# A two-block transformer step on one core: the conditioning products moved to TensorE, the first norm done by token, the last bias joined to the expert products, and an earlier next block

## The reference, cut to what matters

```python
mod = silu(c) @ w_ada + b_ada                      # one row of 6 * 1024, six parts
h = rms(x, norm_mix) * (1 + sc_m) + sh_m           # needs sh_m, sc_m: the first 2048 columns
proj = h @ w_in                                    # q, kv, q_i, k_i, w_i, z, xbc, dt, gates
mixed = sigmoid(g_attn) * y_attn + sigmoid(g_ssd) * y_ssd
x = x + g_m * (mixed @ w_out)
h = rms(x, norm_ffn) * (1 + sc_f) + sh_f
# 32 experts, 4 per token: for each row of a block of expert e
out = act(xb @ w_gu[e] + b_gu[e]) @ w_dn[e] + b_dn[e]
x = x + g_f * sum over the token's experts of gate * out
```

## Time and profile before

| what | value |
|---|---|
| three runs | 2173.53, 2178.62, 2182.28 us; median 2178.62 us |
| the profiled execution, its own time | 2177.95 us |
| its span, from the first to the last instruction | 2176.1 us |
| mean granted TensorE clock | 0.966 |
| busy: PE, PEld, DVE, ACT, POOL | 1990.9, 1168.7, 679.1, 368.4, 75.7 us |
| moved by DMA | 583.21 MB, 268 GB/s over the span |

### The profile page before, as it was taken

The page is one execution under the profiler, slowest core; times in us unless marked ns, Lnnn a source line. Parts: engine busy times, 40 slices in busy tenths (PEclk is TensorE's granted clock), DMA queues, the critical chain, the costliest instruction groups (busy, mean ns, idle before and its releaser), DMA issues.

```text
span 2176.1 us, 22293 instructions
## 1 busy us (share of the span) xinstructions
PE 1990.9 (91%) x8838; PEld 1168.7 (54%) x8838; DVE 679.1 (31%) x1352; ACT 368.4 (17%) x747; POOL 75.7 (3%) x132
## 2 busy tenths in 40 slices
PE   3987899899998998988999898898999999999998
PEld 2774786533333333333333333566788547668863
DVE  6499541422221112211122221252333015423321
ACT  1122311201010000000010100233211023422110
POOL 0000000000000000000000000110000011000000
PEclk8998989799999999999999999899999999999999
DMA  9674424499999999999999996452444332334441
GB/s 355 208 246 177 154 78 177 190 399 427 427 427 428 428 428 428 428 428 427 428 429 427 428 428 286 174 187 84 163 150 150 132 140 94 138 119 152 155 155 39
DMA packets 135538, 583.21 MB, mean 268 GB/s; under 512 B 9432, under 2 KB 55640, under 8 KB 110640
## 3 DMA queue, kind: packets, MB, share of 16 engines
q1 hardware_dynamic: 131424, 575.87, 66.3%
q0 software_dynamic: 4048, 6.42, 1.4%
HBM read 579.64 MB, written 2.62 MB: 268 GB/s over the span
## 4 chain that ended last, share of the span: by engine, by line
PE 58%; DMA 30%; DVE 8%; ACT 2%; issue 2%; SPq 1%; PEldq 0%; DVEq 0%; PEld 0%; ACTq 0%
PE psum L351 45%; DMA work<-w_gu 17%; DMA work<-w_dn 9%; PE psum L561 8%; PE psum L604 4%; DVE work L1363 2%; DMA ring<-w_gu 1%; DMA ring<-w_dn 1%; DMA ring<-w_ada 1%; PE psum L1877 1%; DVE work L1565 1%; DMA ring<-w_in 1%; SPq L455 0%; PE psum L932 0%; DVE work L1535 0%
## 5 line engine op out<-in xcount | busy, mean ns | idle before, releaser
L351 PE MATMUL psum<-normed,ring 128*128 128x256 f32 (+1 forms) x2432 | 507.9, 371 | 4.9 <-DMA ring<-w_in 4.9
L351 PEld LDWEIGHTS psum<-normed,ring 128*128 128x128 f32 x2432 | 444.3, 192 | 65.3 <-DMA ring<-w_in 5.2
L561 PE MATMUL psum<-ring,normed 128*64 128x512 f32 x1024 | 236.6, 617 | 33.5 <-DMA ring<-w_gu 33.5
L561 PE MATMUL psum<-work,normed 128*64 128x512 f32 x1024 | 234.2, 612 | 33.9 <-DMA work<-w_gu 33.9
L351 PE MATMUL psum<-ring,work 128*128 128x512 f32 x560 | 242.3, 593 | 4.7 <-DVE work L2477 2.7
L351 PE MATMUL psum<-work 128*128 128x128 f32 (+8 forms) x1192 | 202.8, 349 | 21.2 <-issue 10.8
L351 PEld LDWEIGHTS psum<-work 128*128 128x128 f32 (+3 forms) x1192 | 149.6, 198 | 83.4 <-issue 62.2
L351 PE MATMUL psum<-ring,normed 128*128 128x512 f32 (+2 forms) x416 | 173.7, 575 | 13.4 <-DMA ring<-w_in 5.5
L561 PEld LDWEIGHTS psum<-ring,normed 128*64 128x64 f32 x1024 | 81.9, 142 | 187.9 <-issue 187.9
L561 PEld LDWEIGHTS psum<-work,normed 128*64 128x64 f32 x1024 | 81.6, 141 | 185.3 <-issue 185.3
L351 PEld LDWEIGHTS psum<-ring,work 128*128 128x128 f32 x560 | 105.9, 190 | 134.8 <-issue 132.7
(11 more groups left out here) (290 smaller groups left out, 1317.5 us busy)
## 6 DMA issues: line engine op xcount, KB each, us to landing
ring<-w_gu SPq DMA_DIRECT2D x64, 2048.0 KB, 27.1
work<-w_gu SPq DMA_DIRECT2D x64, 2048.0 KB, 27.2
ring<-w_dn SPq DMA_DIRECT2D x32, 2048.0 KB, 27.4
work<-w_dn SPq DMA_DIRECT2D x32, 2048.0 KB, 27.3
ring<-w_in SPq DMA_DIRECT2D x25, 2048.0 KB, 12.6
ring<-w_up SPq DMA_DIRECT2D x44, 1024.0 KB, 6.5
ring<-w_ada SPq DMA_DIRECT2D x12, 2048.0 KB, 15.9
ring<-w_down SPq DMA_DIRECT2D x10, 2048.0 KB, 7.8
```

Of the source, the lines that this page charges most:

```text
L351: return pe.matmul(out, lhsT, rhs, start=first, stop=last, **kw)
L561: ins = pe.matmul(b[r], self.hgT[:, 2 * q + k, r], ws[e][:, k, n0:n0 + 512], start=False, stop=q == QUARTERS - 1 and k == 1, skip_group_ch ...
```

## The change

- The 12 parts of `w_ada` are multiplied on PE: `ada(j)` makes eight products with `cond` as the stationary operand, 32 columns wide (one column is `cond`, the others are zero), the product of block k in rows 32 * (k mod 4) of one bank. ACT evicts the 128 x 512 result to `acc`, and `sum_mod` or `mod_rows` adds over the partitions as before. Parts 2, 3, 0, 1 come first. `sum_first` puts all four sums into one bank, which DVE evicts once. PE waits for its own products before it signals the slot used.
- The first norm goes by token: `x` is loaded once, ahead of `w_ada`, and stays; ACT and DVE scale it, PE turns it into four banks, and ACT and DVE evict the banks with scale and shift to `h`. `xT`, `sum_squares` and `inverse_root` are gone.
- `dt` is computed with the index weights (88 columns instead of 72); its own product is gone. The index scores, the masks and the picking of tile 0 go over 128 keys.
- PE's order: the gates `ga` 0 and 1 and both halves of `z` 1 are put between the logits and the attention of tile 1; the other gates go between the parts of the state-space part. The orders of ACT and of both lists are changed to match. DVE scales `y` of tile 0 before it starts on tile 1.
- `x1` waits for `mixed` by pairs of blocks. The ranks are counted by tile, in three banks. The rows of a pair are announced in two halves.
- `GT`, `yb`, and their four scalings and additions are gone. Each pair has two more products of two rows, `b_dn`, that start the banks of the down product; POOL loads these rows, two DMAs for each pair, after the earlier pair's down product.
- `params2` and the gate weights of the second block are loaded earlier, the router weights too.
- SP starts on the second block's weights when the last pair's up product is done; ACT starts its first squares by parts of `x` as they are added.

The core of the diff (the list of banks, declarations, and renumbered semaphore values are left out):

```diff
-    s = [("ada", j) for j in range(4)]
-    s += [("win", 0), ("win", 1), ("ada", 4), ("win", 2), ("ada", 5), ("win", 3), ("ada", 6), ("wkv",), ("win", 4)]
-    s += [("ada", 7), ("win", 5), ("win", 6), ("ada", 8), ("win", 7), ("ada", 9), ("gate", 0), ("ada", 10)]
-    s += [("gate", 1), ("ada", 11), ("gate", 2), ("gate", 3), ("wo",), ("wso", 0), ("wso", 1)]
+    s = [("ada", j) for j in ADA_FIRST]
+    s += [("win", 0), ("win", 1), ("win", 2), ("win", 3), ("ada", 4), ("wkv",), ("win", 4), ("ada", 5), ("win", 5)]
+    s += [("win", 6), ("ada", 6), ("gate", 0), ("win", 7), ("ada", 7), ("ada", 8), ("gate", 1), ("ada", 9), ("gate", 2)]
+    s += [("gate", 3), ("ada", 10), ("wo",), ("ada", 11), ("wso", 0), ("wso", 1)]
...
+ADA_FIRST = (2, 3, 0, 1)
...
+        pool.wait_ge(*earlier(("dn", 1 - u, 1)))
+        for dh in range(2):
+            pool.dma_start(self.b_dn[32 * dh:32 * dh + 2, :], io["b_dn"][bass.ds(2 * p, 2), 512 * dh:512 * dh + 512])\
+                .then_inc(self.down_bias_in, 16)
...
-            if j == 1:
-                for bank in range(2):
-                    act.wait_ge(*B.released(*(("hg",) + tag + (bank,)), it=it))
-                act.nop().then_inc(self.rows_ready, 1)
+            act.wait_ge(*B.released(*hg, it=it))
+            act.nop().then_inc(self.rows_ready[j], 1)
...
+        pe.wait_ge(self.down_bias_in, it * 32 * TWINS + 32 * (u + 1))
         for dh in range(2):
             pe.wait_ge(*B.empty("dn", u, dh, it=it))
+            pe.matmul(psum[:, B.no(("dn", u, dh))], mem.consts_rows("pair_row", 32 * dh), self.b_dn[32 * dh:32 * dh + 2, :],
+                      start=True, stop=False, skip_group_check=True)
...
+    mem.x_part = lambda t, j: BP.released("y", TWINS - 1, t, j, it=PAIRS // TWINS - 1)
...
+        sp.dma_start(x, io["x"].rearrange("(t p) d -> p t d", p=P)).then_inc(x_in, 16)
...
+            sp.wait_ge(*BP.ready("u", TWINS - 1, 1, it=ROUNDS * (PAIRS // TWINS) - 1))
+        sp.wait_ge(*BP.ready("u", TWINS - 1, 1, it=PAIRS // TWINS - 1))
...
+        def ada(j):
+
+            w = wait_slot("ada", j)
+            pe.wait_ge(*B.empty("a", j))
+            for k in range(KC):
+                g = k % 4
+                ins = matmul(pe, bank("a", j)[32 * g:32 * g + 32], cond[:, k], w[:, k], k < 4, k >= 4)
+            ins.then_inc(*B.fills("a", j))
+            pe.wait_ge(*B.ready("a", j))
+            pe.nop().then_inc(ada_done, 1)
...
-        sum_mod(0)
-        sum_squares(1, sig[:, 0:KC])
-        for j in range(1, 4):
-            sum_mod(j)
+        def first_transposes(i):
+
+            pe.wait_ge((x1n_left, x1n_right)[i // 2], NT)
+            transposes(("xh", i), [xh[:, t, k * P:(k + 1) * P] for k in (2 * i, 2 * i + 1) for t in range(NT)])
+
+        pe.wait_ge(cond_ready, 1)
+        for i in range(3):
+            first_transposes(i)
+        ada(2)
+        ada(3)
+        first_transposes(3)
+        sum_first(0)
+        ada(0)
+        sum_first(1)
+        ada(1)
+        sum_first(2)
+        sum_first(3)
...
-        mod_rows(5)
+        ada(4)
...
-        pe.wait_ge(*B.empty("dt"))
-        pe.wait_ge(narrow_in, 16)
-        for t in range(NT):
-            for k in range(KC):
-                ins = matmul(pe, bank("dt")[:, t * SH:(t + 1) * SH], h[:, k, t * P:(t + 1) * P], w_dt[:, k], k == 0, k == KC - 1)
-        ins.then_inc(*B.fills("dt"))
-        sum_mod(7)
+        mod_rows(5)
...
+        logits(0)
+        by_token(("z", 0), wait_slot("win", 6), 0, 512)
+        ada(6)
+        attend(0)
+        logits(1)
+        w = wait_slot("gate", 0)
+        by_feature(("ga", 0), w, 0)
+        sum_mod(6)
+        by_feature(("ga", 1), w, 256)
+        by_token(("z", 1), wait_slot("win", 7), 0, 512)
+        ada(7)
+        attend(1)
...
+        ada(8)
...
+        sum_mod(8)
+        gate = gates(1)
+        gate(0)
+        gate(1)
...
+        ada(9)
...
+        gate = gates(2)
+        gate(0)
+        sum_mod(9)
+        gate(1)
         intra(1)
-        w = wait_slot("gate", 3)
-        by_feature(("ga", 6), w, 0)
-        by_feature(("ga", 7), w, 256)
+        gate = gates(3)
+        gate(0)
+        ada(10)
+        gate(1)
         pe.wait_ge(*S.ready("wo"))
         pe.wait_ge(*B.released("O", 1))
-        w = slot(S.no(("wo",)), 4, 1024)
-        for p in range(4):
-            by_feature(("ya", p), w, 256 * p, attnT, 4)
-        for t in range(NT):
-            pe.wait_ge(y_ready, t + 1)
-            for j in range(2):
-                transposes(("yT", t, j), [y_tok[:, t, (4 * j + c) * P:(4 * j + c + 1) * P] for c in range(4)])
+        attn_out((0, 1))
+        y_transposes(0)
+        mod_rows(10)
+        attn_out((2,))
+        ada(11)
+        attn_out((3,))
+        mod_rows(11)
+        y_transposes(1)
...
-        pe.wait_ge(mixed_ready, 1)
...
+                if (t, j) == (0, 0):
+                    pe.wait_ge(mixed_ready, k // 2 + 1)
...
+        counts(("cum", 0), K("tri_le"), 0, True, True).then_inc(*B.fills("cum", 0))
+        counts(("cum", 1), ones, 0, True, False)
+        counts(("count",), ones, 0, True, False)
+        pe.wait_ge(mask_ready, 2)
+        counts(("cum", 1), K("tri_le"), 1, False, True).then_inc(*B.fills("cum", 1))
+        counts(("count",), ones, 1, False, True).then_inc(*B.fills("count"))
...
-        pe.wait_ge(gates_ready, 1)
-        transposes(("GT",), [X.gate[:, t, 0:E] for t in range(NT)])
         pe.wait_ge(weights_ready, 1)
-        pe.wait_ge(*B.released("GT"))
-        pe.wait_ge(bdn_in, 16)
-        for t in range(NT):
-            for j in range(2):
-                pe.wait_ge(*B.empty("yb", t, j))
-                matmul(pe, bank("yb", t, j), X.gateT[0:E, t * P:(t + 1) * P], X.b_dn[0:E, j * 512:(j + 1) * 512])\
-                    .then_inc(*B.fills("yb", t, j))
...
+        def ada_rows(out, j):
+            take(out, bank("a", j), "a", j)
+            act.wait_ge(*B.released("a", j))
+            act.nop().then_inc(ada_in, 1)
+
+        step(act.activation(rms[:, 0, 0:1], prm("eps"), ACT.Sqrt))
+        for t in range(NT):
+            mean_root(t, t + 1, z[:, 0, 0:512], lambda j: (x_in, 16))
+            act.activation(xh[:, t, 0:512], x[:, t, 0:512], ACT.Copy, scale=rms[:, t, 1:2]).then_inc(x1n_left, 1)
+        for n, j in enumerate(ADA_FIRST):
+            ada_rows(acc_first[:, n], j)
...
+        exponents(0)
+        z_half(0)
+        ada_part(6)
+        attend(0)
+        conv_silu(range(6))
+        gate(0)
+        exponents(1)
+        gate(1)
+        conv_silu(range(6, NX))
+        z_half(1)
+        ada_part(7)
+        attend(1)
...
-        def product(j):
-
-            dve.wait_ge(*S.ready("ada", j))
-            if j >= 3:
-                dve.wait_ge(*B.ready("m", j - 3))
-            w, a = slot(S.no(("ada", j)), KC, 512), acc[:, j % 3]
-            step(TS(a, w[:, 0], cond[:, 0:1], None, ALU.mult))
-            for k in range(1, KC):
-                ins = STT(out=a, in0=w[:, k], scalar=cond[:, k:k + 1], in1=a, op0=ALU.mult, op1=ALU.add)
-                if k < KC - 1:
-                    step(ins)
-            signal(ins, ada_sum, j + 1)
...
+        for i in (1, 3):
+            dve.wait_ge(*B.ready("xh", i))
+            for c in range(2):
+                k = 2 * i + c
+                TS(h[:, k], bank("xh", i)[:, c * L:(c + 1) * L], a1[:, k:k + 1], mod[:, k:k + 1], ALU.mult, ALU.add)\
+                    .then_inc(h1_ready[1], 1)
...
-            if t == 0:
-                take_mod(6)
-                product(7)
...
-        for t in range(NT):
-            for j in range(2):
-                v = x[:, t, j * 512:(j + 1) * 512]
-                dve.wait_ge(*B.ready("yb", t, j))
-                take(TT(X.out[:, j], bank("yb", t, j), gain[:, j * 512:(j + 1) * 512], ALU.mult), "yb", t, j)
-                step(TT(v, v, X.out[:, j], ALU.add))
...
-        sp.wait_ge(mem.moe_done, 1)
...
-                    act.wait_ge(mem.x_ready, 1)
+                    act.wait_ge(*mem.x_part(t, j))
```

434 lines of the change are left out of this document (217 added, 217 removed).

## The result

The changed kernel takes **2124.04 us** (median of four runs, 2116.14 to 2126.80), the kernel before 2176.07 on the same chip (four runs, 2172.86 to 2182.28): the ratio is 0.9752, with a 95% interval of 0.9726 to 0.9778, so 52 us less. Forecast were 2139 and a range of 2126 to 2157: the direction was right, the gain was larger than the range allowed by 2 us. The profiled spans are 2122.5 and 2176.1 us.

What follows compares the result with a forecast made beforehand. Experts bound by weight DMA, the front by PE and DVE in turn, the second block by PE. Terms -8.2 - 12.1 - 2.0 - 10.6 - 6.9 = -39.8 gave 2139 us; own range 2132 to 2146, wider range 2126 to 2157.

Steps and rivals of the forecast that it cites:

- The step that failed: First q product to `ys`: the granted clock recovers a quarter of 7.7 us lost in long products, -2.0 us.
- the clock comes back whole: Rival: all 7.7 us of clock return instead of 2, and about 2 in the first expert quarter; 2131 us, chance 0.10.
- PE's work from q to `ys`: First q product to `ys`: PE's busy time goes from 258.9 to 273.5 us, eight `ada` products adding 18.4.
- the lower end, 1.7: Bound for one `w_ada` part on PE: four products perfectly at once, 6.9 / 4; the forecast took 2.3 us.
- Idle time: First q product to `ys`: PE's idle time falls from 32.7 us to 6 us.
- The rival of new waits in the queues of ACT and DVE: Reordered in-order queues make PE wait; half the idle time stays, +10 to +14 us, 2151 us; chance 0.15.
- The start: Kernel start to first q product: 37 us instead of 45.2, -8.2 us.
- the end of the front: 336.8 us to first pair: earlier `x1`, gathering sooner, pair starting right behind gathering; -10.6 us.
- the start's second path: Before the first q product: fourth `w_ada` part's landing, product, evictions and sum; said to end at 35.5 to 38 us.
- The expert stage: Pairs of experts: bound by weight loads, 919 us at 428 GB/s, unchanged; getting longer would show the prediction wrong.
- The slack: Each expert pair: PE has 6 us to spare under the weight loads, covering the added `b_dn` products.
- The hand-over: Experts to second block: weights no longer last, first product after DVE's last addition at 1363.8 instead of 1370.67; -6.9 us.

Runs made afterwards that it cites:

- `bias_x4`: The changed kernel with each of the two `b_dn` products of a pair made four times (same result): 2161.43 us, ratio 0.9926.

## Why the prediction was wrong, point by point

**The step that failed** is "Of the clock, 0.82 to 0.95 in these stages, I expect some back as idle time goes; long products there run at 15.3 to 16.5 us instead of 14, 7.7 us in all: I take a quarter, -2.0". In its place the runs show -16.9 us in this stretch and -5.2 behind it. The mechanism was right in the main, its size was not, twice over. The 7.7 counted the long products alone; by shape, the same products took 1.5 (128x256) + 2.9 (128x512) + 3.1 (transposes) + 5.9 (64 columns) + 1.8 (row sums) + 1.7 (`O`) = **16.9 us** less. Three quarters of it lie in short products, because those stand right behind the waits: they are what the wait was for. (The first logits are the exception: there the clock fell as the wait began.) And there was no reason for a quarter: with the waits down to 7.8 us, three of five stages stand at 1.00. Even the rival in which "the clock comes back whole" (2131) was priced with 7.7 and about 2 for the first quarter of the experts. Filling the waits of the kernel before, with nothing else changed, gave 14.6 us back; resting the changed kernel for 13.0 us cost 9.2.

The same step was left out behind `ys`: -15.2 instead of -10.6. `ys` takes 27.89 us for 29.58, the second router product 2.40 for 3.29, gathering 5.54 for 6.28, the last turning 1.07 for 1.95 and the first bias products 1.14 for 2.09: 5.2 us, all of them clock.

**PE's work from q to `ys`** was foretold at 273.5 less 2.0 and measured at 250.8. 16.9 of that is the clock, and 8 x (2.3 - 1.92) = 3.0 the part of `w_ada`: right in its kind (four quarters at once, as the rows' quarters), and nearer the lower end, 1.7, than the row I took. Of the 2.8 that remain, 0.8 is the index projection, which takes 3.7 us with 88 columns as with 72, and 0.8 the scores of tile 0 (8.5 us before, 6.7 now, in part by the clock); the rest is small. At the start one part took 3.59 us, at a granted clock of 0.53.

**Idle time** was 7.8 us for 6: what had been named (evictions ahead of `O`, the last `yT`, 1.9 us) and one load of 1.9 us, plus 2.3 for PE's waits for its own `ada` products, which the text had put into the price. The rival of new waits in the queues of ACT and DVE did not come.

**The start**, -8.1 for -8.2, and the end of the front up to the clock's share were right: the pair starts 2.1 us behind gathering. That is read from the traces; no run took these steps back one by one. Two sums of the prediction are off by a little: 424.66 - 417.15 is 7.5 and not 7.6, and the start's second path adds up to 35.2 to 38.5 and not 35.5 to 38. Neither moves the forecast.

**The expert stage** was said to have a fixed length, and one longer than before was named as a sign of being wrong. It has +2.2. "The twelve loads of 2.10 MB take 58.8 us" left out what else the DMA engines carry: 8 KB more for a pair cost 0.35 us of each, 5 to 6 us in all, partly made up for by a first pair at the full clock (the first slots are free 378.15 - 371.03 = 7.1 us after its start, for 9.95 before). The text had looked at what stands behind the new wait in POOL's queue, which is not where it costs. The slack was put at 6 us for a pair from the 51.5 of the second one; over the stage PE is busy 54.9 of 59.5, so it is 4.5.

**The hand-over**, -6.0 for -6.9: weights are not last any more, as foretold. PE starts 7.3 us after the last product. In later profiles of the changed kernel PE itself is what ends the wait, 5.15 us behind its last product, with ACT's output there before: reading the flag once, ahead of the loop, brought DVE's reciprocal forward by 0.9 us (from 2.6 us behind PE's last product to 1.7) and the first product by 0.2 (7.8 to 7.6).

**The sum**: -39.8 was foretold and -53.6 came, 13.8 more. Of the -23.5 of surprise between q and the first pair 14.9 + 5.2 = 20.1 are clock; against it stand +2.2 in the expert stage, +0.9 in the hand-over and +6.4 in the second block, the clock behind one wait in each layer, which varies from execution to execution (the four runs lie between 2116.14 and 2126.80).

## What to carry to other kernels

Where PE's granted clock is under 1.00, price a removed wait at more than its length: here 1.7 us for each microsecond of three waits of 3.6 to 5 us, 1.3 for one of 18, found by comparing the ns of one product **by shape** in slow and in full stretches, short shapes above all. Look also for products of few rows or few columns that stand in a row: the clock fell in them here though PE never waited. Ask of a stage that is bound by DMA what the small loads cost in it: 24 KB in six loads cost 0.7 us among 25 MB, more than their bytes, and loading the whole table once gave back 11 to 13 us, 9 of them in the experts. Moving work off the engine that others wait for and reordering the work of the one that waits are worth more together (33 us) than the first alone (20, by one quick profile) or the second alone (8).

## What the runs showed of the hardware that was not expected

- The order of the products doesn't matter for running side by side: 0, 1, 2, 3, then 0, 1, 0, 1 and 0, 0, 1, 1 all take 1.92 to 1.95 us for sixteen instructions; one quarter alone takes 7.05. That is 3.7 times as fast. The Trainium skill (TensorE: Matmul & The Clock Gate, The mechanism) lets weight loads overlap only where the row group differs and has the products start strictly in the order of the program; the first is contradicted by 1.92 us. Under the second, with two products of two instructions each in one quarter one behind the other, the order 0, 0, 1, 1 would take over 5 us by the 0.43 us of a single one: that is an estimate, and 1.94 speaks against it. The starts in the trace do too. With the order 0, 0, 1, 1 the sixteen instructions of the part at 122.10 us start in four groups of four, at 122.10 to 122.15, 122.56 to 122.60, 122.99 to 123.03 and 123.42 to 123.46, and in one quarter alone they start 0.43 us apart; so each group has one of each quarter.
- The granted clock falls to 0.50 in the middle of work without a wait when that work is narrow: in `bias_x4` in the two-row products of every one of the sixteen pairs, with PE busy throughout, and with DVE relieved behind the 16-column `dt` product and the one-column sums, within 7.1 us in which PE is busy throughout (0.88 over them).
- The clock behind one and the same wait (3.28 us) was full in one execution and low in another, with nothing changed. A difference of 3 us in one stage of one profile is no finding until a second profile has it.
- Small loads by POOL's queue lengthen a pair by 0.30 us for 8 KB in two loads of two partitions (59.48 - 59.18), by 0.28 when these are one load (59.46 - 59.18), and by 0.40 for 16 KB in four (59.18 - 58.78). 8 KB are 0.02 us at 428 GB/s. What they hold up was not tried. The Trainium skill (DMA: Bandwidth & Descriptors, Why a DMA increments its semaphore by 16 and not by 1) takes the number of engines from a transfer's slowest dimension, the largest number up to 16 that divides it, which would be two for two partitions, and names an exception for some transfers of GpSimd's; no run here shows which engines carried these.
- Products of two rows and of 32 rows take the same time, 0.64 us each and 1.06 us for four of them.
